# Chunked attention on one core: the order of one head's scores, a unit of values and the softmax steps in the first head of each later group

## The chip, the core and the metric

The kernel runs on one core of a Trainium2 chip. The core has five engines with their own instruction streams: TensorE (PE in the profile, its weight loads PEld) multiplies matrices into PSUM banks, VectorE (DVE) and ScalarE (ACT) read and write PSUM and SBUF, GpSimd (POOL) works on SBUF only, and SyncE (SP) issues most transfers. The engines wait for each other by semaphores. The metric is the device time of one execution in microseconds, as the median of several runs.

## What is computed

Two model blocks follow each other on 512 positions of width 1024. The second one ends with an attention layer of 16 heads of 64 columns and an MLP. Only the attention layer is touched:

```python
q, k, v = jnp.split(h @ w_in, 3, axis=-1)          # 16 heads of 64 columns
def one_chunk(c):                                   # 64 queries, band of 576 keys
    s = jnp.einsum('bqhd,bkhd->bhqk', qb, kb).astype(jnp.float32) * scale + bias[None]
    s = jnp.where(valid[None, None, None, :], s, -jnp.inf)
    p = jax.nn.softmax(s, axis=-1).astype(vb.dtype)
    return jnp.einsum('bhqk,bkhd->bqhd', p, vb)
...
return o @ w_out
```

## The kernel before

The program is one hand-ordered instruction list for each engine; no planner orders anything. It has six phases (a mixer, a gated FFN, retention, an MLP, attention, an MLP). Every fp32 matrix product is done as three matmuls on halves: high by high, low by high, high by low (L629 to L631, helper `product`). ScalarE makes the high half of a block of weights (`w_hi`, L1101) and GpSimd the low half (`w_lo`, L605).

In the attention phase the heads go in four groups of four. A *unit* is a stretch of such products on TensorE: a qk unit gives 128 columns of q or k (24 matmuls of 512 columns), a v unit gives values for half of the positions (48 matmuls of 256 columns). The units of the next group are spread over the heads of the current one, and between them stand three smaller pieces for each head:

- `scores(h + 1)` on TensorE (L973, L975): four tiles of scores, two matmuls each, in the order 0, 2, 3, 1. Tile 0 first waits until the scores of head h have been taken. Tile 1 goes to bank 6 and first waits (semaphore `pt_ready`) until VectorE has finished the low halves of the transposed probabilities of head h - 1 (`probs_lo`), since their source is in bank 6.
- `mix(h - 1)` on TensorE (L1002, L1004), the probabilities of head h - 1 times the values.
- `turn(h)` on TensorE (L991), ten transposes of the probabilities of head h. The last two go to bank 6 and wait until VectorE has taken the scores of head h + 1.

VectorE does `maxima` (L2191, L2195: adds the bias, takes the row maximum), `normalise` (L2199, L2204), `probs_lo` (L2210, `probs_t_lo` in the profile), takes over each unit (`qk_taken` L1790, `qk_lo` L2181, for values `value_lo` L2164), adds the mixed halves (`mixed_add` L2215) and makes their low half (`mixed_lo` L2221). ScalarE does `exps` (L1482), `probs_hi` (L1491), `qk_hi` (L1446, L1447), the high half of the values in `v_unit` (L1472), `mixed_copy` (L1497), `mixed_hi` (L1502) and the weights' high halves. With `normalise(h + 1)` and `exps(h + 1)` in the list of head h, `probs_lo(h)` comes after both.

Each head h has one turn in the loops. The first head of a later group (h = 4, 8 and 12; `s == 0` in the code) has two units, the last qk unit and the first v unit; the second head has the second v unit and a qk unit, the third and fourth have one qk unit each. In the last group, output units (`unit4_narrow`, L629 with `hid_hi`) take the place of the qk units. `unit4_narrow` starts only when every unit before it has been taken.

Of the kernel before, what the change touches and what calls it, by code (L numbers as in the profile page):

```python
# [163 lines left out]
def build(nc, phases, x_in, w_in, w_out, w_gate, w_up, w_down, ret_w_in, ret_w_out, att_w_in,  # L164
# [4 lines left out]
    with ctx:  # L169
# [453 lines left out]
        def _(pe):  # L623
# [213 lines left out]
            for f in phases:  # L837
# [108 lines left out]
                if f == "att":  # L946
# [7 lines left out]
                    def unit4_narrow(n):  # L954

                        unit4(H, 0, fresh=0, bank0=0)
# [64 lines left out]
                    for h in range(1, ATT_HEADS):  # L1021
                        s, last_group = h % 4, h >= ATT_HEADS - 4
                        if s == 0:
                            qk_unit(3)
                            unit_v(X)
                            scores(h + 1)
                            mix(h - 1)
                            turn(h)
                            continue
                        if s == 1 and h > 1:  # L1030
                            unit_v(X)
                            v_units = c.unit.n
                        if last_group and s == 1:
                            scores(h + 1)
                            pe.wait_ge(mix_ready, 8)
                            unit4_narrow(s - 1)
                        else:
                            if last_group:
                                unit4_narrow(s - 1)
                            else:  # L1040
                                qk_unit(s - 1)
                            if h + 1 < ATT_HEADS:
                                scores(h + 1)
                        if s == 1:
                            pe.wait_ge(unit_taken, v_units)
                        mix(h - 1)
                        turn(h)
# [16 lines left out]
        def _(act):  # L1064
# [173 lines left out]
            for f in phases:  # L1238
# [193 lines left out]
                if f == "att":  # L1432
# [89 lines left out]
                    for h in range(1, ATT_HEADS):  # L1522
                        s, last_group = h % 4, h >= ATT_HEADS - 4
                        if s == 0:
                            qk_unit(3)
                            mixed_copy(h - 1)
                            v_unit(0)
                            exps(h + 1)
                            probs_hi()
                            mixed_hi(h - 1)  # L1530
                            continue
                        if s == 1 and h > 1:
                            v_unit(1)
                        if last_group and s == 1:
                            exps(h + 1)
                            after_unit()
                            mixed_copy(h - 1)
                        else:
                            if last_group:
                                after_unit()  # L1540
                            else:
                                qk_unit(s - 1)
                            mixed_copy(h - 1)
                            if h + 1 < ATT_HEADS:
                                exps(h + 1)
                        probs_hi()
                        mixed_hi(h - 1)
# [15 lines left out]
        def _(dve):  # L1563
# [257 lines left out]
            for f in phases:  # L1821
# [330 lines left out]
                if f == "att":  # L2152
# [99 lines left out]
                    for h in range(1, ATT_HEADS):  # L2252
                        s, last_group = h % 4, h >= ATT_HEADS - 4
                        if s == 0:
                            qk_taken(3)
                            maxima(h + 1)
                            qk_lo(3)
                            mixed_add(h - 1)
                            value_lo()
                            normalise(h + 1)  # L2260
                            probs_lo()
                            mixed_lo(h - 1)
                            continue
# [89 lines left out]
```

## Time and profile before

| what | us |
|---|---|
| median of 3 runs | 1879.1 (1878.47 to 1879.91) |
| the profiled execution | 1879.74 |
| its span in the trace | 1878.0 |
| attention's first matmul piece on scores to its last mix | 1307 to 1501 |

The profile is of one execution. A timeline row gives the start, the duration, the engine, the source line, the operation with what it writes and reads, and in brackets how long the engine was idle before it and what ended that. Starts of matmuls that follow each other without a wait are closer than their durations, since matmuls overlap: the distance of two starts is what a matmul costs TensorE, and 128x256 ones start 0.12 us apart, 128x512 ones 0.23 us apart.

### The profile page before, as it was taken

The page shows a single profiled execution, that of the slowest core. Times are in us where ns is not written, and L with a number is a line of the kernel's source. Part 1 is how long each engine was busy: PE and PEld are TensorE (multiplying, and loading weights), DVE is VectorE, ACT ScalarE, POOL GpSimd, SP SyncE. Part 2 cuts the span into 40 slices and gives each one's busy share as a digit, 9 for nine tenths or more (in the row PEclk, how much of TensorE's full clock was granted, in tenths as well). Part 3 has the DMA queues.
Part 4 walks back from the last instruction along what each step waited for, and adds up shares of the span by engine and source line. Part 5 has one row for each costly group of instructions (what it writes and reads, how often), then busy time and mean ns, then how long its engine had stood idle before and what let it go on. Part 6 is the DMA issues. An engine that isn't in the chain of part 4 may idle for free.

```text
span 1878.0 us, 25366 instructions
## 1 busy us (share of the span) xinstructions
PE 1851.3 (99%) x10114; PEld 1608.1 (86%) x10114; DVE 1131.9 (60%) x1807; ACT 848.9 (45%) x1319; POOL 945.9 (50%) x408
## 2 busy tenths in 40 slices
PE   8999999999999999999999999999999999999997
PEld 6778889898888888888889899898888889898987
DVE  5997775775776333433665545357877766354455
ACT  5335443342354232333454535445666546444453
POOL 4573466475443434433347566574223338475653
PEclk9999999999999999999999999999999999999998
DMA  5222414424232222222244141413333252422301
GB/s 185 90 90 68 136 66 144 159 72 154 68 113 68 94 87 90 82 78 88 90 157 135 46 155 48 148 31 118 83 107 106 79 174 74 135 91 90 133 3 45
DMA packets 143041, 186.66 MB, mean 99 GB/s; under 512 B 4016, under 2 KB 102592, under 8 KB 142800
## 3 DMA queue, kind: packets, MB, share of 16 engines
q1 hardware_dynamic: 134848, 170.67, 27.8%
q10 hardware_dynamic: 8080, 14.44, 2.7%
q8 instruction: 77, 1.26, 0.3%
q14 instruction: 36, 0.29, 0.0%
HBM read 178.76 MB, written 6.33 MB: 99 GB/s over the span
## 4 chain that ended last, share of the span: by engine, by line
PE 83%; DVE 8%; ACT 2%; issue 1%; ACTq 0%; DVEq 0%
PE ps L629 27%; PE ps L631 27%; PE ps L630 27%; DVE ps L1852 1%; ACT work L1482 1%; DVE diagonals L1607 1%; DVE xl L1633 0%; DVE work L2204 0%; DVE probs_t_lo L2210 0%; DVE work L2191 0%; PE ps L991 0%; DVE work L1790 0%; PE ps L925 0%; ACT w_hi L1101 0%; DVE q_hi L2181 0%
## 5 line engine op out<-in xcount | busy, mean ns | idle before, releaser
L605 POOL TENSOR_TENSOR w_lo<-raw,w_hi 128x1024 fp32r<-128x1024 f32 x228 | 553.0, 2431 | 752.7 <-ACT w_hi L1101 752.7
L629 PE MATMUL ps<-xh,w_hi 128*128 128x512 f32 x1408 | 554.7, 394 | 3.4 <-DVE xl L1633 1.3
L631 PE MATMUL ps<-xh,w_lo 128*128 128x512 f32 x1408 | 548.7, 390 | 0.0
L630 PE MATMUL ps<-xl,w_hi 128*128 128x512 f32 x1408 | 548.6, 390 | 0.0
L1101 ACT ACTIVATE w_hi<-raw 128x1024 fp32r<-128x1024 f32 x248 | 259.7, 1057 | 409.0 <-PE ps L631 400.8
L629 PEld LDWEIGHTS ps<-xh,w_hi 128*128 128x128 f32 x1408 | 264.7, 188 | 62.8 <-issue 8.0
L631 PEld LDWEIGHTS ps<-xh,w_lo 128*128 128x128 f32 x1408 | 264.5, 188 | 55.8
L630 PEld LDWEIGHTS ps<-xl,w_hi 128*128 128x128 f32 x1408 | 264.9, 188 | 55.3 <-issue 1.9
L629 PE MATMUL ps<-hid_hi,w_hi 128*128 128x256 f32 (+1 forms) x944 | 300.8, 319 | 1.9 <-DVE att_v L2164 0.8
L631 PE MATMUL ps<-hid_hi,w_lo 128*128 128x256 f32 (+1 forms) x944 | 299.5, 317 | 0.0
L630 PE MATMUL ps<-hid_lo,w_hi 128*128 128x256 f32 (+1 forms) x944 | 299.4, 317 | 0.0
L629 PEld LDWEIGHTS ps<-hid_hi,w_hi 128*128 128x128 f32 x944 | 179.9, 191 | 14.9 <-DVE hid_lo L1796 1.8
L631 PEld LDWEIGHTS ps<-hid_hi,w_lo 128*128 128x128 f32 x944 | 179.9, 191 | 12.0
L630 PEld LDWEIGHTS ps<-hid_lo,w_hi 128*128 128x128 f32 x944 | 180.0, 191 | 11.8 <-issue 0.2
L1761 DVE TENSOR_TENSOR x<-x,ps 128x512 f32<-128x512 f32 x140 | 94.9, 685 | 124.9 <-PE ps L631 124.9
L605 POOL TENSOR_TENSOR w_lo<-down,w_hi 128x1024 fp32r<-128x1024 f32 x40 | 96.4, 2424 | 79.3 <-ACT w_hi L1101 79.3
L631 PE MATMUL ps<-combined,w_lo 128*128 128x256 f32 x480 | 135.8, 283 | 0.0
L630 PE MATMUL ps<-combined,w_hi 128*128 128x256 f32 x480 | 135.8, 283 | 0.0
L629 PE MATMUL ps<-combined,w_hi 128*128 128x256 f32 x480 | 135.8, 283 | 0.0
L605 POOL TENSOR_TENSOR w_lo<-work,w_hi 128x1024 fp32r<-128x1024 f32 x52 | 125.0, 2419 | 17.8 <-ACT w_hi L1101 17.8
L2128 DVE SCALAR_TENSOR_TENSOR work<-ps,r_bc 128x512 f32<-128x512 f32 x64 | 43.6, 690 | 83.3 <-PE ps L631 83.2
L629 PEld LDWEIGHTS ps<-combined,w_hi 128*128 128x128 f32 x480 | 92.1, 192 | 0.4
(252 smaller groups left out, 2805.2 us busy)
## 6 DMA issues: line engine op xcount, KB each, us to landing
raw<-in_mlp_w_dram SPq DMA_DIRECT2D x32, 1024.0 KB, 5.3
raw<-in_ret_w_in_dram SPq DMA_DIRECT2D x24, 1024.0 KB, 5.1
work<-in_mlp_w_dram SPq DMA_DIRECT2D x24, 1024.0 KB, 6.3
raw<-in_att_w_in_dram SPq DMA_DIRECT2D x12, 1024.0 KB, 5.4
raw<-in_w_gate_dram SPq DMA_DIRECT2D x11, 1024.0 KB, 5.4
raw<-in_w_up_dram SPq DMA_DIRECT2D x11, 1024.0 KB, 5.4
raw<-in_w_in_dram SPq DMA_DIRECT2D x10, 1024.0 KB, 5.1
raw<-in_ret_w_out_dram SPq DMA_DIRECT2D x8, 1024.0 KB, 5.1
```

The source lines that it names most:

```text
L605: nc.gpsimd.tensor_tensor(halves_of(wl[:, b % 2, :], half), halves_of(source, half), halves_of(wh[:, b % 2, :], half).bitcast(F32), ALU.su ...
L629: nc.tensor.matmul(o, a[0], b[0], start=first, stop=False, skip_group_check=True)
L630: nc.tensor.matmul(o, a[0], b[1], start=False, stop=False, skip_group_check=True)
L631: return nc.tensor.matmul(o, a[1], b[0], start=False, stop=last, skip_group_check=True)
L1101: nc.scalar.activation(halves_of(wh[:, slot, :], half), source, ACT.Copy).then_inc(w_hi, c.made(w_hi))
L1482: last = nc.scalar.activation(probs[:, h % 2, cut], probs[:, h % 2, cut], ACT.Exp, bias=nmx[:, i:i + 1], accum_out=rs[:, i:i + 1])
L1607: V.reciprocal(rough, root_rows).then_inc(dve_step, c.made(dve_step))
L1761: V.tensor_tensor(tiles, tiles, ps[:, where, :].rearrange("p (m c) -> p m c", m=2), ALU.add).then_inc(unit_taken, c.made(unit_taken))
L1852: V.scalar_tensor_tensor(total if last else acc, src, w, acc, ALU.mult, ALU.add).then_inc(signal, c.made(signal))
L2128: V.scalar_tensor_tensor(hval[:, u % 2, :], bank(), 0.0, r_bc[:, :], ALU.max, ALU.mult).then_inc(unit_taken, c.made(unit_taken))
```

## The change

In the turn of the first head of a later group, `scores(h + 1)` moves on TensorE from behind the v unit to between the qk unit and the v unit. On ScalarE `exps(h + 1)`, with the two bias loads that it issues where there is a head h + 5, moves ahead of `mixed_copy(h - 1)` and `v_unit(0)`. On VectorE `normalise(h + 1)` moves ahead of `mixed_add(h - 1)` and `value_lo()`. No instruction is added or removed. It applies to h = 4, 8 and 12.

```diff
@@ tensor @@
                         if s == 0:
                             qk_unit(3)
+                            scores(h + 1)
                             unit_v(X)
-                            scores(h + 1)
                             mix(h - 1)
                             turn(h)
@@ scalar @@
                             qk_unit(3)
+                            exps(h + 1)
                             mixed_copy(h - 1)
                             v_unit(0)
-                            exps(h + 1)
                             probs_hi()
@@ vector @@
                             qk_taken(3)
                             maxima(h + 1)
                             qk_lo(3)
+                            normalise(h + 1)
                             mixed_add(h - 1)
                             value_lo()
-                            normalise(h + 1)
                             probs_lo()
```

TensorE before, in the turn of head 4, from the end of the v unit (L631) over the scores of head 5 (`k_odd`, `q_lo` are the tiles that hold an odd head's k and q) to the first matmul of the mix of head 3:

```order
L631 MATMUL ps<-w_hi,xl 128x256
L973 MATMUL ps<-k_odd,q_lo 128x128 [waits s_taken]
L975 MATMUL ps<-k_odd,q_lo 128x128
L973 MATMUL ps<-k_odd,q_lo 128x384
L975 MATMUL ps<-k_odd,q_lo 128x384
L973 MATMUL ps<-k_odd,q_lo 128x512
L975 MATMUL ps<-k_odd,q_lo 128x512
L973 MATMUL ps<-k_odd,q_lo 128x256 [waits pt_ready]
L975 MATMUL ps<-k_odd,q_lo 128x256
L1002 MATMUL ps<-probs_t_hi,att_v 128x512 [waits pt_ready,mix_added]
```

TensorE after, in the same turn, from the end of the qk unit (L631 with 512 columns) to the start of the v unit (L629 with 256):

```order
L631 MATMUL ps<-xh,w_lo 128x512
L973 MATMUL ps<-k_odd,q_lo 128x128 [waits s_taken]
L975 MATMUL ps<-k_odd,q_lo 128x128
L973 MATMUL ps<-k_odd,q_lo 128x384
L975 MATMUL ps<-k_odd,q_lo 128x384
L973 MATMUL ps<-k_odd,q_lo 128x512
L975 MATMUL ps<-k_odd,q_lo 128x512
L973 MATMUL ps<-k_odd,q_lo 128x256 [waits pt_ready]
L975 MATMUL ps<-k_odd,q_lo 128x256
L629 MATMUL ps<-w_hi,xh 128x256 [waits unit_taken,w_lo]
```

The eight matmuls and their two waits stand 48 matmuls earlier, and the whole v unit now stands behind them.

VectorE before, in the same turn, from the negated maxima of head 5 (L2195) to the low halves of the transposed probabilities of head 4 (L2210):

```order
L2195 TENSOR_SCALAR cols<-cols 128x4 [waits s_taken]
L2181 TENSOR_TENSOR k_parts<-work,k_parts 64x512 [waits unit_taken,hi_made]
L2181 TENSOR_TENSOR k_odd<-work,k_odd 64x512
L2215 TENSOR_TENSOR work<-ps,work 64x512 [waits mix_copied]
L2164 SCALAR_TENSOR_TENSOR att_v<-ps,cols,att_v 128x4x64 [waits hi_made,unit_done]
L2164 SCALAR_TENSOR_TENSOR att_v<-ps,cols,att_v 128x4x64
L2199 RECIPROCAL cols<-cols 128x4 [waits curve_made]
L2204 TENSOR_SCALAR work<-work,cols 128x128 [waits dve_step]
L2204 TENSOR_SCALAR work<-work,cols 128x256
L2204 TENSOR_SCALAR work<-work,cols 128x384
L2204 TENSOR_SCALAR work<-work,cols 128x512
L2210 TENSOR_TENSOR probs_t_lo<-ps,probs_t_hi 128x512 [waits hi_made] x2
```

VectorE after, the same stretch:

```order
L2195 TENSOR_SCALAR cols<-cols 128x4 [waits s_taken]
L2181 TENSOR_TENSOR k_parts<-work,k_parts 64x512 [waits unit_taken,hi_made]
L2181 TENSOR_TENSOR k_odd<-work,k_odd 64x512
L2199 RECIPROCAL cols<-cols 128x4 [waits curve_made]
L2204 TENSOR_SCALAR work<-work,cols 128x128 [waits dve_step]
L2204 TENSOR_SCALAR work<-work,cols 128x256
L2204 TENSOR_SCALAR work<-work,cols 128x384
L2204 TENSOR_SCALAR work<-work,cols 128x512
L2215 TENSOR_TENSOR work<-ps,work 64x512 [waits mix_copied]
L2164 SCALAR_TENSOR_TENSOR att_v<-ps,cols,att_v 128x4x64 [waits hi_made,unit_done]
L2164 SCALAR_TENSOR_TENSOR att_v<-ps,cols,att_v 128x4x64
L2210 TENSOR_TENSOR probs_t_lo<-ps,probs_t_hi 128x512 [waits hi_made] x2
```

The five instructions of `normalise` stand three places earlier, ahead of the two steps that wait for the mix and the v unit. All that precedes L2195 on VectorE, `probs_lo(3)` among it, stands where it stood.

## Rows read from the trace of the kernel before

**Rows 1.** The page, part 1: busy time, share of the span and instructions by engine.
```profile
PE 1851.3 (99%) x10114; PEld 1608.1 (86%) x10114; DVE 1131.9 (60%) x1807; ACT 848.9 (45%) x1319; POOL 945.9 (50%) x408
```

**Rows 2.** The page, part 4: the chain that ended last, shares by engine.
```profile
PE 83%; DVE 8%; ACT 2%; issue 1%; ACTq 0%; DVEq 0%
```

**Rows 3.** Waits of PE, 1300 to 1520 us: total us, times, longest us.
```profile
PE ps L991 <- DVE cols L2191: 2.3, 7, 0.5
...
PE ps L973 <- DVE probs_t_lo L2210: 0.7, 2, 0.4
```

**Rows 4.** Timeline of PE, head 1: scores of head 2, then the mix.
```profile
1322.99 0.22 PE L973 MATMUL ps<-k_parts,q_hi 128*128 128x128 f32 x1
...
1324.50 0.39 PE L973 MATMUL ps<-k_parts,q_hi 128*128 128x256 f32 x1 [0.31 <-DVE probs_t_lo L2210]
...
1324.85 0.40 PE L1002 MATMUL ps<-probs_t_hi,att_v 128*128 128x512 f32 x1
```

**Rows 5.** Timeline of DVE in the same stretch: `probs_lo(0)`.
```profile
1322.83 1.62 DVE L2210 TENSOR_TENSOR probs_t_lo<-ps,probs_t_hi 128x512 fp32r<-128x512 f32 x3
```

**Rows 6.** Timeline of PE, head 4: starts of v unit, scores and mix.
```profile
1352.88 0.28 PE L629 MATMUL ps<-w_hi,xh 128*128 128x256 f32 x1
...
1358.63 0.23 PE L973 MATMUL ps<-k_odd,q_lo 128*128 128x128 f32 x1
...
1359.90 0.39 PE L1002 MATMUL ps<-probs_t_hi,att_v 128*128 128x512 f32 x1
```

**Rows 7.** Timeline of DVE, end of head 3's turn, head 4's, start of head 5's.
```profile
1350.87 2.78 DVE L2181 TENSOR_TENSOR q_lo<-work,q_lo 64x512 fp32r<-64x512 f32 x1
1353.67 0.18 DVE L2199 RECIPROCAL cols<-cols 128x4 f32<-128x4 f32 x1
...
1355.08 1.61 DVE L2210 TENSOR_TENSOR probs_t_lo<-ps,probs_t_hi 128x512 fp32r<-128x512 f32 x3
...
1357.21 0.68 DVE L1790 SCALAR_TENSOR_TENSOR work<-ps,r_bc 128x512 f32<-128x512 f32 x1
1359.51 0.29 DVE L2191 CUSTOM_DVE_ANT_0 work<-ps,work 128x128 f32<-128x128 f32 x1 [1.63 <-PE ps L975]
...
1373.66 0.69 DVE L1790 SCALAR_TENSOR_TENSOR work<-ps,r_bc 128x512 f32<-128x512 f32 x1 [3.52 <-PE ps L631]
```

**Rows 8.** Timeline of POOL and ACT there, and L2181's durations (ns, min/median/max).
```profile
1347.88 5.22 POOL L605 TENSOR_TENSOR w_lo<-raw,w_hi 128x1024 fp32r<-128x1024 f32 x2 [17.96 <-ACT w_hi L1101]
...
1350.89 0.71 ACT L1482 ACTIVATE work<-work,cols 128x512 f32<-128x512 f32 x1
...
L2181 DVE TENSOR_TENSOR q_lo<-work,q_lo x8: 687/688/2782, 1297.2 to 1449.5; 64x512 fp32r<-64x512 f32 x8
```

**Rows 9.** Timelines of PE (v unit's start) and DVE (`probs_lo(7)`), head 8.
```profile
1402.22 0.28 PE L629 MATMUL ps<-w_hi,xh 128*128 128x256 f32 x1
...
1404.43 1.61 DVE L2210 TENSOR_TENSOR probs_t_lo<-ps,probs_t_hi 128x512 fp32r<-128x512 f32 x3
```

**Rows 10.** Timelines of ACT, DVE and PE, head 13: second v unit taken, output unit.
```profile
1466.88 0.84 ACT L1472 ACTIVATE att_v<-ps,cols 128x256 fp32r<-128x256 f32 x2 [1.22 <-PE ps L631]
...
1467.94 0.88 DVE L2164 SCALAR_TENSOR_TENSOR att_v<-ps,cols,att_v 128x256 fp32r<-128x256 f32 x2
...
1468.96 0.47 PE L629 MATMUL ps<-hid_hi,w_hi 128*128 128x512 f32 x1 [0.85 <-DVE att_v L2164]
```

**Rows 11.** PE's timeline at both ends; last row: one microsecond's busy times and PEclk.
```profile
12.68 0.76 PE L629 MATMUL ps<-xh,w_hi 128*128 128x512 f32 x1 [1.27 <-DVE xl L1633]
...
15.73 0.58 PE L629 MATMUL ps<-xh,w_hi 128*128 128x512 f32 x1
...
1861.66 1.05 PE L753 MATMUL ps<-ones,sum_of_squares 128*128 128x1 f32 x8 [1.57 <-DVE sum_of_squares L1648]
...
1862.00:1863.00 1.00, 1.00 (x10) 1.00 (x9) 0.00 (x0) 0.97 (x3) 0.00 (x0) 0.87 0.00 0
```

## Prediction

> **What bounds the kernel now.** I read the page's busy times first: TensorE is busy for 1851.3 us, 99% of the span, and VectorE for 60% [rows 1]. The chain that ended last agrees, 83% of it being TensorE [rows 2]. So the time changes where TensorE starts or stops waiting, and what VectorE and ScalarE win by themselves is worth nothing. Next the waits of TensorE in the attention phase. Its engine rows give small ones only: 2.3 us in seven waits of the transposes for the maxima, and 0.7 us in two waits of the fourth score tile for `probs_lo` [rows 3]. The reader should look at the second kind, because it is the wait that the change moves. Then the timelines of the stretches around heads 4, 8 and 12. In the turn of head 4 TensorE runs v unit, scores and mix without a wait: 1352.88, 1358.63, 1359.90 [rows 6].
>
> **How the wait on bank 6 is priced.** In the turn of head 1 the scores stand directly behind one qk unit, as the change now has it for heads 4, 8 and 12. They start at 1322.99, their last pair is held until 1324.50, and the mix starts at 1324.85 [rows 4]. What it waited for is `probs_lo(0)`, which started at 1322.83 and took 1.62, so ended at 1324.45 [rows 5]. Two things follow. The last pair of `scores(h + 1)` can't start before `probs_lo(h - 1)` ends, and what stands behind the scores starts 0.40 us after that end. Without a wait the scores cost 1359.90 - 1358.63 = 1.27 us [rows 6].
>
> **TensorE, the scores moved up.** In the turn of head 4 the scores wait for `probs_lo(3)`. That one starts at 1355.08 and ends at 1356.69 [rows 7]. Before, the scores started at 1358.63, and the v unit of 1358.63 - 1352.88 = 5.75 us hid this completely. After the change they start where the v unit started, at 1352.88 [rows 6], and `probs_lo(3)` is still 3.8 us from its end. Nothing ahead of it moves: the turn of head 3 and the two steps in head 4's list before the moved ones are unchanged on all engines. So the v unit starts at 1356.69 + 0.40 = 1357.09 instead of at 1352.88 + 1.27 = 1354.15, and the mix at 1362.84 instead of 1359.90. **Cost: 2.94 us.** In the turn of head 8 `probs_lo(7)` ends at 1404.43 + 1.61 = 1406.04 and the v unit started at 1402.22 [rows 9]: 1406.44 - 1403.49 = 2.95 us. The third group repeats the pattern to within 0.01 us. Sum: 2.94 + 2.95 + 2.94 = **8.8 us**.
>
> **Why `probs_lo(3)` is so late there.** `qk_lo`'s second instruction, ahead of it on VectorE, takes 2.78 us against a median of 0.69, while GpSimd works on two `w_lo` halves from 1347.88 to 1353.10 [rows 7, 8]. This long form is there in all three groups, so I take the long value; the rival below takes the short one.
>
> **The other first wait of the scores**, for the scores of head 4 to be taken, costs nothing: VectorE took them before it made `q_lo` at 1350.87 [rows 7]. What is queued behind the new wait on TensorE is the v unit, the mix of head 3, the transposes of head 4 and everything after; ScalarE's copy of the mixed half and of the values, VectorE's `value_lo` and `probs_lo(4)` wait for these, and come later by the same 2.9 us.
>
> **VectorE and ScalarE, the softmax steps moved up.** VectorE was idle for 1.63 us before the maxima of head 5 at 1359.51, waiting for the scores [rows 7]. After the change the scores are complete some 0.4 us after 1356.69, before `qk_taken` is over at 1357.21 + 0.68 = 1357.89, so the maxima start 1.6 us earlier. `exps(5)` and `normalise(5)` then run while TensorE is in the v unit. Their cover is that unit, which ends at 1362.84. Had they no cover, they would still not be on TensorE's path, because `turn(5)` needs them a whole head later. The two bias loads that `exps` issues on ScalarE's queue are issued earlier, and are used four heads later: nothing. The steps that the softmax passes, `mixed_add(3)` and `value_lo`, wait for the mix and the v unit, which are now 2.9 us later than before, so they don't lose by standing behind. GpSimd's and SP's lists are the same, and what they wait for (`w_hi` after the qk unit, `qk_lo`) is not behind anything moved.
>
> **Is anything paid back?** VectorE is ahead after head 4, but it waits 3.52 us for TensorE at 1373.66, in head 5's turn [rows 7]. From there both keep the same distance as before, and the small waits of heads 6 and 7 stay. The one place where the lead counts is head 13. There the output unit starts at 1468.96 after an idle 0.85 us, because the second v unit must be taken first. ScalarE's part of that ends at 1466.88 + 0.84 = 1467.72, VectorE's starts at 1467.94 because it was busy until then [rows 10]. After the change VectorE has finished the previous head earlier and is free at 1467.72 (as times of before); it starts about 0.05 later, so the gain is 0.17 us, once. At the least it is 0, at the most the whole idle 0.85.
>
> **Sum.** 8.8 - 0.2 = +8.7 us (from unrounded terms). The profiled execution took 1879.74 us with a span of 1878.0; its span becomes 1886.7. It lies 0.6 above the median of the runs shown, so I add the difference to the median: 1879.1 + 8.7 = **1887.8 us**, 0.46% slower.
>
> **Rival 1: TensorE's clock falls in the new waits.** Each leaves TensorE idle for about 2.7 us, from the sixth score matmul to the seventh. The longest idle before a dense stretch in the attention phase is now 0.85. At the end of the program the granted clock went from the 2.4 GHz level towards the 1.2 GHz level (0.87 in the microsecond from 1862) after 1.57 us of idleness and one microsecond of one-column matmuls [rows 11]. That is nearly as long, so I can't exclude it. Price: after the start TensorE worked at the lower level from 12.68 to 15.73 [rows 11], 3.05 us, half of which is lost: 1.5 us for each fall. One to three falls give 1889.3 to 1892.3. Against it: the idle stretch lies between full ones, and the one at the end didn't.
> The Trainium skill says in "TensorE: Matmul & The Clock Gate", Part 1, that the array's clock is gated by how busy TensorE has been; it would speak for this rival if the wait counts as idleness enough, and the sum would be by it what this rival says.
>
> **Rival 2: the held instruction is free.** If GpSimd's work no longer met `q_lo` (2.78 to 0.69), VectorE would next wait for the exponentials, whose last one ends at 1350.89 + 0.71 = 1351.60 and its accumulator some 0.1 later [rows 8]. The reciprocal would come at about 1351.8 instead of 1353.67, and `probs_lo` 1.9 us earlier [rows 7]. Cost per group 1.0, sum 3.1 - 0.2: 1882.0 us, too little to be told from no change. Against it: neither engine's work is moved ahead of that point.
> The Trainium skill, "SBUF — State Buffer", section "Who interferes with whom", says that GpSimd and a VectorE instruction with two SBUF inputs exclude each other for the whole instruction, and that whoever starts first holds the port. The trace agrees in the length of `q_lo`. By that rule the order of starts decides, so a small shift of GpSimd could turn it; this is the same 1882.0.
>
> **Rival 3, not slower: the wait at bank 6 finds its data ready.** The place is L973's fourth tile. If the count that it waits for were reached by `probs_lo(2)`, or `probs_lo(3)` ended before about 1353.9, nothing would be held, and only the 0.17 of head 13 would be left: 1878.9 us. The point from which the result could be told from no change (0.2% or 3.8 us, about what a measurement of this kernel can tell) is 1.3 us lost per group, thus `probs_lo(3)` ending at 1355.1 instead of 1356.69. Against it: the code counts heads 0 to h - 1 for the scores of h + 1, and the wait of head 1 ended 0.05 us after `probs_lo(0)` did [rows 4, 5].
> For a real gain the waits of the transposes for the maxima would have to go too, and no more than 2.3 us of them exist [rows 3].
>
> **Chances.** Forecast 0.76 (1886.5 to 1889), rival 1 0.12, rival 2 0.06, rival 3 0.06 (0.02 of it with a gain). Slower by over 0.2%: 0.76 + 0.12 + 0.02 (a rival 2 with only some groups free) = 0.90; within: 0.04 + 0.04 = 0.08; faster 0.02. The range takes in the forecast with a reach of 2 us down for the 0.40 and the restart, and most of rival 1: 1885.5 to 1891.5.
>
> **What the profile of the changed kernel would show.** Right: in the turns of heads 4, 8 and 12 the fourth tile of the scores (L973, 128x256) starts 2.8 us behind its neighbour, released by `probs_t_lo` L2210, and the PE waits for L2210 grow by about 8 us in three waits; the maxima of heads 5, 9 and 13 follow `qk_taken` without idleness; the v unit has no wait before it but this one. Rival 1: PEclk below 1.00 right behind those waits, and 512-column matmuls that start further apart than before. Rival 2: `q_lo` at 0.69 in heads 3, 7 and 11. Rival 3: no PE wait there. The forecast is wrong if `probs_lo(3)` doesn't end at 1356.7, or if the transposes of head 4 start waiting, which I expect not.

## The result

The changed kernel is slower. Before, the median of 4 runs is 1879.51 us (1878.47 to 1880.65); changed, it is 1891.56 us (1889.5 to 1893.55, 4 runs). The ratio is 1.0062, with a 95% interval from 1.0051 to 1.0074: 12 us more. The forecast was 1887.8 us with a range of 1885.5 to 1891.5, so the sign is right and the size is 3.8 us short; the median lies 0.06 us above the range, and as a rise above the kernel before (12.05 us, where the range stood for 6.4 to 12.4) inside it. The executions of the changed kernel also spread more than those before: 4.1 us against 2.2.

The profiled execution took 1889.5 us with a span of 1887.7. Its page, parts 1 and 4 (busy time, share of the span and instructions; then the shares of the chain that ended last):

```profile
PE 1852.3 (98%) x10114; PEld 1608.6 (85%) x10114; DVE 1128.2 (60%) x1807; ACT 849.2 (45%) x1319; POOL 948.2 (50%) x408
...
PE 83%; DVE 8%; ACT 2%; issue 1%; ACTq 0%; DVEq 0%
```

TensorE's busy time grew by 1.0 us against [rows 1] and the span by 9.7, so nearly all of the loss in this execution is TensorE not working. Its waits over the whole execution (total us, times, longest us):

```profile
PE ps L973 <- DVE probs_t_lo L2210: 8.6, 5, 2.7
...
PE ps L991 <- DVE cols L2191: 2.4, 7, 0.5
```

The wait of the fourth score tile for `probs_lo` went from 0.7 us in two times to 8.6 in five; the waits of the transposes stayed [rows 3]. The timeline of TensorE in the turn of head 4 (start, us, engine, line, operation, and in brackets the idle time before it):

```profile
1353.49 0.22 PE L973 MATMUL ps<-k_odd,q_lo 128*128 128x128 f32 x1
...
1354.30 0.40 PE L975 MATMUL ps<-k_odd,q_lo 128*128 128x512 f32 x1
1357.38 0.38 PE L973 MATMUL ps<-k_odd,q_lo 128*128 128x256 f32 x1 [2.68 <-DVE probs_t_lo L2210]
...
1357.71 0.28 PE L629 MATMUL ps<-w_hi,xh 128*128 128x256 f32 x1
```

The v unit starts at 1357.71, which is 4.22 us after the scores' start at 1353.49 where 1.27 would do without a wait [rows 6]: 2.95 us lost. The same wait is 2.67 us long in heads 8 and 12. VectorE's timeline shows what it waited for:

```profile
1351.49 2.78 DVE L2181 TENSOR_TENSOR q_lo<-work,q_lo 64x512 fp32r<-64x512 f32 x1
1354.31 0.18 DVE L2199 RECIPROCAL cols<-cols 128x4 f32<-128x4 f32 x1
...
1355.71 1.61 DVE L2210 TENSOR_TENSOR probs_t_lo<-ps,probs_t_hi 128x512 fp32r<-128x512 f32 x3
1357.24 0.67 DVE L2221 TENSOR_TENSOR hid_lo<-work,hid_hi 64x512 fp32r<-64x512 f32 x1
1357.84 0.68 DVE L1790 SCALAR_TENSOR_TENSOR work<-ps,r_bc 128x512 f32<-128x512 f32 x1
1358.44 0.27 DVE L2191 CUSTOM_DVE_ANT_0 work<-ps,work 128x128 f32<-128x128 f32 x1
```

These are [rows 7], some 0.63 us later, as TensorE's rows are here too. `probs_lo(3)` ends at 1357.32, and TensorE goes on 0.06 later. The maxima of head 5 now follow `qk_taken` without the 1.63 us of idleness.

The second part of the loss stands behind the wait of head 8. TensorE's timeline from there, with the v unit's 256-column matmuls:

```profile
1409.64 0.39 PE L973 MATMUL ps<-k_odd,q_lo 128*128 128x256 f32 x1 [2.67 <-DVE probs_t_lo L2210]
...
1409.98 0.28 PE L629 MATMUL ps<-w_hi,xh 128*128 128x256 f32 x1
...
1410.33 0.34 PE L629 MATMUL ps<-w_hi,xh 128*128 128x256 f32 x1
1410.46 0.42 PE L630 MATMUL ps<-w_lo,xh 128*128 128x256 f32 x1
1410.67 0.42 PE L631 MATMUL ps<-w_hi,xl 128*128 128x256 f32 x1
...
1413.86 0.28 PE L631 MATMUL ps<-w_hi,xl 128*128 128x256 f32 x1
1413.98 0.28 PE L629 MATMUL ps<-w_hi,xh 128*128 128x256 f32 x1
...
1417.21 0.40 PE L1002 MATMUL ps<-probs_t_hi,att_v 128*128 128x512 f32 x1
```

Matmuls start 0.12 us apart at first, then 0.21 from 1410.46 on, and 0.12 again from 1413.86. One microsecond of each, as busy times of the engines, then the granted clock (the third number from the end):

```profile
1409.00:1410.00 1.00, 0.36 (x3) 0.36 (x4) 1.00 (x3) 0.00 (x0) 0.00 (x0) 1.00 0.01 4
...
1411.00:1412.00 1.00, 1.00 (x7) 1.00 (x7) 1.00 (x5) 0.99 (x2) 0.00 (x0) 0.50 0.00 0
```

So the clock fell from the 2.4 to the 1.2 GHz level after TensorE had idled 2.67 us. The v unit, from its start at 1409.98 to the first matmul behind it at 1417.21, took 7.23 us instead of 5.75: 1.48 us. In heads 4 and 12 of this execution it did not fall.

**A measure without the ends of the program.** The start of the program and its last sixteen microseconds vary by themselves from execution to execution. To compare traces I take the time from the first matmul of the attention phase to the first one-column matmul at the end; before, the two starts are 1276.76 (below) and 1861.66 [rows 11], 584.90 us. There is one trace of the kernel before, so this reference is a single execution. First before, then two of the changed kernel:

```profile
1276.76 0.47 PE L629 MATMUL ps<-xh,w_hi 128*128 128x512 f32 x1 [0.87 <-issue]
```

```profile
1277.59 0.47 PE L629 MATMUL ps<-xh,w_hi 128*128 128x512 f32 x1 [0.87 <-issue]
...
1872.43 1.05 PE L753 MATMUL ps<-ones,sum_of_squares 128*128 128x1 f32 x8 [1.57 <-DVE sum_of_squares L1648]
```

Changed, that is 594.84 us: 9.94 more, of which 1.48 are the fall of the clock and 8.46 the rest. The forecast's sum for the rest was 8.66. The table has every profiled kernel read in this way; "falls" are the v or output units of which a part ran at the lower level in that trace. The last column takes off what that cost: in a v unit its length above 5.75 us (1.48 in most), in the output unit of head 13 its length above that of the run with the normalising alone (1.6 with the softmax steps alone, 1.85 with the exponentials alone).

| kernel | median us (its before) | attention's start to end part, against 584.90 | falls seen | without them |
|---|---|---|---|---|
| the change | 1891.56 (1879.51) | +9.94 | 1 | +8.46 |
| the change again | 1892.65 (1879.55) | +11.54 | 2 | +8.58 |
| wait filled with work | 1887.52 (1879.55) | +8.53 | 0 | +8.53 |
| scores alone | 1890.30 (1879.55) | +9.99 | 1 | +8.5 |
| softmax steps alone | 1881.83 (1879.55) | +3.80 | 1 | +2.2 |
| three tiles alone | 1879.59 (1880.20) | -0.04 | 0 | -0.04 |
| probs_lo first | 1884.80 (1880.20) | +4.17 | 0 | +4.17 |
| longer wait | 1895.63 (1880.20) | +16.43 | 3 | +12.0 |
| mixed_lo deferred | 1875.45 (1880.20) | -3.43 | 0 | -3.43 |
| probs_lo first, filled | 1885.40 (1879.92) | +4.40 | 0 | +4.40 |
| exponentials alone | 1886.34 (1879.92) | +6.65 | 1 | +4.8 |
| normalising alone | 1881.39 (1879.92) | +2.17 | 0 | +2.17 |
| probs_lo first, again | 1885.04, one execution (1879.57) | +4.25 | 0 | +4.25 |

### The profile page after: what moved, and what is told of

Its sections match the earlier page's. It is cut to its first block, busy times and chain, and to the rows that moved or that the text cites. A ratio compares the mean times of both kernels' runs of the same rounds, so it can differ in the third digit from the quotient of the medians.

```text
span 1887.7 us, 25366 instructions
## 1 busy us (share of the span) xinstructions
PE 1852.3 (98%) x10114; PEld 1608.6 (85%) x10114; DVE 1128.2 (60%) x1807; ACT 849.2 (45%) x1319; POOL 948.2 (50%) x408
## 4 chain that ended last, share of the span: by engine, by line
PE 83%; DVE 8%; ACT 2%; issue 1%; ACTq 0%; DVEq 0%
PE ps L629 27%; PE ps L630 27%; PE ps L631 27%; DVE ps L1852 1%; DVE probs_t_lo L2210 1%; DVE work L2204 1%; ACT work L1482 1%; DVE diagonals L1607 1%; DVE xl L1633 0%; PE ps L991 0%; PE ps L925 0%; DVE work L2191 0%; ACT w_hi L1101 0%; DVE work L1790 0%; DVE q_hi L2181 0%
## 5 line engine op out<-in xcount | busy, mean ns | idle before, releaser
L629 PE MATMUL ps<-xh,w_hi 128*128 128x512 f32 x1408 | 554.6, 394 | 4.3 <-DVE xl L1633 2.1
L631 PE MATMUL ps<-xh,w_lo 128*128 128x512 f32 x1408 | 548.6, 390 | 0.0
L629 PEld LDWEIGHTS ps<-xh,w_hi 128*128 128x128 f32 x1408 | 264.8, 188 | 63.5 <-issue 8.0
L631 PEld LDWEIGHTS ps<-xh,w_lo 128*128 128x128 f32 x1408 | 264.7, 188 | 55.4
L629 PE MATMUL ps<-hid_hi,w_hi 128*128 128x256 f32 (+1 forms) x944 | 300.8, 319 | 1.8 <-DVE att_v L2164 0.7
L631 PE MATMUL ps<-hid_hi,w_lo 128*128 128x256 f32 (+1 forms) x944 | 299.5, 317 | 0.0
L629 PEld LDWEIGHTS ps<-hid_hi,w_hi 128*128 128x128 f32 x944 | 179.9, 191 | 14.8 <-DVE hid_lo L1796 1.8
L631 PEld LDWEIGHTS ps<-hid_hi,w_lo 128*128 128x128 f32 x944 | 179.9, 191 | 12.0
L631 PE MATMUL ps<-combined,w_lo 128*128 128x256 f32 x480 | 135.8, 283 | 0.0
L629 PE MATMUL ps<-combined,w_hi 128*128 128x256 f32 x480 | 135.8, 283 | 0.0
L629 PEld LDWEIGHTS ps<-combined,w_hi 128*128 128x128 f32 x480 | 92.1, 192 | 0.4
```

The lines of the kernel that those rows point to most:

```text
L629: nc.tensor.matmul(o, a[0], b[0], start=first, stop=False, skip_group_check=True)
L631: return nc.tensor.matmul(o, a[1], b[0], start=False, stop=last, skip_group_check=True)
```

## The experiments

**The change again, and with the waits filled.** The first question was whether the 3.8 us above the forecast are the clock. The changed kernel was run again, and beside it a version in which TensorE multiplies into a bank that is free there while it waits:

```diff
+                            if i == 1 and filled:
+                                pe.wait_ge(mix_added, h - 2)
+                                for _ in range(filled):
+                                    nc.tensor.matmul(ps[:, 7, :], q[:, 0:P], k_hi[:, 0:SEQ],
+                                                     start=True, stop=True, skip_group_check=True)
                             if i == 1 and h >= 2:
                                 pe.wait_ge(pt_ready, pt_before_att + len(TURNED) * (h - 1))
...
                             qk_unit(3)
-                            scores(h + 1)
+                            scores(h + 1, filled=11)
```

> The change again, beside the runs of the kernel before. Theory A (each of three waits on bank 6 costs TensorE 2.9 us, and in some executions the granted clock falls in one to three of them, at 1.5 us each): 1888 to 1893 us with a spread of several us between executions, lowest near 1888.5, against 1879 to 1880 before. Theory B (the 3.8 us that the result lies above the forecast are a constant cost that the trace doesn't show): all executions within 1.5 us of each other, near 1891.5.

Measured: 1892.65 us (1889.16 to 1895.26, 5 runs), ratio 1.0067 [1.0053, 1.0081]. The spread of 6.1 us fits theory A and rules B out. This trace has two falls, in the v units of heads 4 and 12 (7.23 and 7.24 us), where the first had one, in head 8. The traced execution is the fastest of its five. The mean granted clock goes with the time: 0.995 and 0.996 at 1889.16 and 1889.66 us, 0.994 at 1892.65 and 1892.66, 0.992 at 1895.26.

> The change, with eleven extra 128x512 matmuls into the free bank 7 on TensorE between the third and the fourth tile of the moved scores, so that TensorE works through the wait instead of idling. The wait for the probabilities is as long as before, so the cost of the wait itself stays. Theory A (the executions above the forecast are falls of the granted clock in the idle waits): no falls, 1887.5 to 1888.5 us, with a spread below 1.5 us, and the clock of the mean execution as high as before. Theory B (the extra is no matter of the clock): the same median as the change itself, within 0.7 us.

Measured: 1887.52 us (1885.99 to 1889.31, 5 runs), ratio 1.0043 [1.0029, 1.0056]. The filled stretch in the turn of head 4, on TensorE (lines are 5 higher in this kernel; L974 is the filler):

```profile
1352.78 0.39 PE L980 MATMUL ps<-k_odd,q_lo 128*128 128x512 f32 x1
1353.01 2.73 PE L974 MATMUL ps<-k_odd,q_lo 128*128 128x512 f32 x11
1355.85 0.38 PE L978 MATMUL ps<-k_odd,q_lo 128*128 128x256 f32 x1
```

The fourth tile comes as late as before, 3.07 us behind its neighbour, but TensorE isn't idle. The granted clock stays at 1.00 over the whole attention phase, all three v units take 5.75 us, and the median falls by 5.1 us, to the forecast; the mean granted clock of its executions is 0.996 or 0.997. The wait's own cost stays, +8.5 us in the trace, so what the filling gives back is time at the lower clock. Its size is less sure: three falls at 1.48 us would be 4.4, not 5.1, and the program's ends are in the medians too. The spread, 3.3 us, is above the 1.5 expected; what it holds is told with the two groups below.

**One part of the change at a time.** TensorE's part alone, that is the diff's first hunk:

> Only TensorE's part of the change: the scores ahead of the v unit; ScalarE and VectorE keep the order of before. Theory A (the wait of the fourth tile is the whole cost and the order of the softmax steps doesn't count): within 0.5 us of the change in the trace, the same three waits of 2.7 us, median 1888 to 1893. Rival (the moved softmax steps cost or give something of their own): over 1 us away from the change.

Measured: 1890.3 us (1889.55 to 1890.86), ratio 1.0055 [1.0041, 1.0069]. The waits in its trace, of which the other two are 2.68 us too:

```profile
1357.97 0.39 PE L973 MATMUL ps<-k_odd,q_lo 128*128 128x256 f32 x1 [2.68 <-DVE probs_t_lo L2210]
```

It loses what the whole change loses (+8.5 us without the fall, against 8.46 and 8.58). The moved scores are the whole cost of the waits, and the moved softmax steps add nothing to it in the traces. The medians are less alike: 1890.3 us with a spread of 1.3 here, against 1892.65 with a spread of 6.1 for the whole change beside it. The waits are as long in both, so whether the softmax steps make the falls more frequent, or five executions are too few, is open.

ScalarE's and VectorE's part alone, that is the other two hunks:

> Only ScalarE's and VectorE's part: exponentials and normalising of head h + 1 ahead of the values' parts; TensorE keeps the order of before. Theory A: no wait of TensorE is added, at most the 0.17 us of head 13 are gained: 1878.9 to 1879.6 us, the same as before. Rival (the part costs something because normalise now blocks mixed_add and value_lo behind it): 1 us or more slower.

Measured: 1881.83 us (1880.52 to 1885.0, 11 runs), ratio 1.0015 [1.0006, 1.0024]: slower by 2.3 us, where I expected no change. Its trace has waits of TensorE that neither other kernel has: 0.25 us before the qk unit of heads 5 and 9, and these two in head 13:

```profile
1470.96 0.39 PE L973 MATMUL ps<-k_parts,q_hi 128*128 128x256 f32 x1 [0.64 <-DVE probs_t_lo L2210]
...
1472.68 0.47 PE L629 MATMUL ps<-hid_hi,w_hi 128*128 128x512 f32 x1 [1.22 <-DVE att_v L2164]
```

One candidate for the reason is in ScalarE's timeline in the turn of head 4. The first row is the first exponential of head 5 with the idle time before it; then come the mixed copy and the values, which are queued behind the exponentials:

```profile
1364.31 0.41 ACT L1482 ACTIVATE work<-work,cols 128x128 f32<-128x128 f32 x1 [2.52 <-DVE cols L2195]
...
1366.63 0.59 ACT L1497 ACTIVATE work<-ps 64x512 f32<-64x512 f32 x1
1367.25 0.84 ACT L1472 ACTIVATE att_v<-ps,cols 128x256 fp32r<-128x256 f32 x2
```

With the scores behind the v unit, the maxima are late, ScalarE idles 2.52 us for them, and the values of the v unit, which the next units wait for, are taken later. The other candidate is VectorE, where the normalising now stands ahead of the values. To see which of the two engines' order costs this, each was moved alone:

> The kernel before with exps(h + 1) ahead of mixed_copy(h - 1) and v_unit(0) on ScalarE in heads 4, 8 and 12, and nothing else moved. It splits the run with the softmax steps alone (2.3 us slower than before), where ScalarE idles 2.5 us for the maxima ahead of exps and mixed_copy and v_unit are queued behind it. Theory A (this queueing on ScalarE is the cost): 1881 to 1882.5 us, as slow as with both parts. Rival (VectorE's part, normalise ahead of mixed_add and value_lo, is the cost): 1879.5 to 1880.3 us, as before.

Measured: 1886.34 us (1885.13 to 1886.88, 6 runs), ratio 1.0034 [1.0021, 1.0046]: 6.4 us slower, far more than either theory said. In its trace `mixed_lo` at the end of head 4's turn, which took 0.69 us, runs while GpSimd works on `w_lo` (1370.93 to 1376.15) and takes 2.80, and VectorE takes the second v unit behind it:

```profile
1371.08 2.80 DVE L2221 TENSOR_TENSOR hid_lo<-work,hid_hi 64x512 fp32r<-64x512 f32 x1
1373.91 0.87 DVE L2164 SCALAR_TENSOR_TENSOR att_v<-ps,cols,att_v 128x256 fp32r<-128x256 f32 x2
```

The same happens in the turn of head 12 (2.75 us). In head 13, where the output unit needs these values at once, TensorE waits 3.28 us, after 1.34 for the fourth score tile. The clock is at the lower level before the second wait is over, and stays there until microsecond 1478:

```profile
1470.74 0.38 PE L973 MATMUL ps<-k_parts,q_hi 128*128 128x256 f32 x1 [1.34 <-DVE probs_t_lo L2210]
...
1474.52 0.77 PE L629 MATMUL ps<-hid_hi,w_hi 128*128 128x512 f32 x1 [3.28 <-DVE att_v L2164]
```

```profile
1472.00:1473.00 1.00, 0.00 (x0) 0.00 (x0) 1.00 (x1) 0.00 (x0) 1.00 (x2) 0.50 0.00 0
```

These two waits, 0.85 before, make 3.8 of the 4.8 us that the table has without the fall. How much of them is the order and how much the long instruction was not told apart.

> The kernel before with normalise(h + 1) ahead of mixed_add(h - 1) and value_lo() on VectorE in heads 4, 8 and 12, and nothing else moved. If ScalarE's queueing is the cost of the softmax steps alone: 1879.5 to 1880.7 us, at most 0.5 us above before. If VectorE's order is the cost: 1881 us or more.

Measured: 1881.39 us (1879.88 to 1884.08, 11 runs), ratio 1.0012 [1.0003, 1.0021]. Its trace has the waits of the softmax run to 0.01 us (0.24 in heads 5 and 9; 0.63 and 1.22 in head 13), with ScalarE's order as before; only the fall behind them is missing. What makes them is on VectorE: it idles for the exponentials, normalises, and takes the first v unit 2.65 us later than before, measured from the transposes of head 4.

```profile
1365.57 0.18 DVE L2199 RECIPROCAL cols<-cols 128x4 f32<-128x4 f32 x1 [1.05 <-ACT work L1482]
...
1367.81 0.88 DVE L2164 SCALAR_TENSOR_TENSOR att_v<-ps,cols,att_v 128x256 fp32r<-128x256 f32 x2
```

So each order costs when it is moved alone, and in each a step that waits was put ahead of steps that free a unit; with both moved the waits are those of VectorE's order.

**The fourth tile by itself.** If the wait on bank 6 is all that costs, the other three tiles can go ahead of the v unit freely:

```diff
-                    def scores(h):
+                    def scores(h, tiles=tuple(SCORES)):
...
-                        for i in SCORES:
+                        for i in tiles:
...
                             qk_unit(3)
+                            scores(h + 1, (0, 2, 3))
                             unit_v(X)
-                            scores(h + 1)
+                            scores(h + 1, (1,))
                             mix(h - 1)
```

> The kernel before, in which three of the four score tiles (0, 2 and 3) of head h + 1 go ahead of the v unit in heads 4, 8 and 12, and only the fourth (tile 1, bank 6) stays behind it; ScalarE and VectorE as before. It differs from the run with the scores alone by that one tile. Theory A (the wait of the tile in bank 6 for probs_lo(h - 1) is the whole cost of moving the scores): no wait of TensorE ahead of the v unit, 1879 to 1880 us, the same as before. Rival (splitting the run of TensorE's work, or the first wait of the scores, costs by itself): over 1 us slower than before.

Measured: 1879.59 us (1879.09 to 1879.88, 11 runs) against 1880.2, ratio 0.9997 [0.9988, 1.0006]; in the trace 0.04 us less than before. Against the scores alone only two matmuls stand elsewhere, and the whole loss is gone.

**Why `probs_lo` is late, and the length of the wait.** The order was changed so that VectorE makes `probs_lo` ahead of the 2.78 us instruction:

```diff
                             mixed_add(h - 1)
+                            if s == 3:
+                                made = c.next(hi_made)
+                                normalise(h + 1)
+                                probs_lo()
+                                qk_lo(s - 1, made=made)
+                                mixed_lo(h - 1)
+                                continue
```

> The change, and in the turns of heads 3, 7 and 11 VectorE normalises head h + 1 and makes probs_lo(h) ahead of the two instructions of qk_lo, of which the second took 2.78 us. Theory A (TensorE waits for the end of probs_lo, which is late because of this instruction): probs_lo ends 1.0 to 1.9 us earlier and the three waits fall from 2.7 to between 0.8 and 1.7 us; 1882 to 1885 us; with idleness that short no fall of the clock, so a spread below 2 us. Rival (probs_lo is late because of what ScalarE does ahead of it): the waits stay above 2.3 us and the time at 1888 or more.

Measured: 1884.8 us (1882.15 to 1885.15, 10 runs), ratio 1.0021 [1.0012, 1.0031]. TensorE's wait in the turn of head 4, and what VectorE does before:

```profile
1355.64 0.39 PE L973 MATMUL ps<-k_odd,q_lo 128*128 128x256 f32 x1 [1.24 <-DVE probs_t_lo L2210]
```

```profile
1352.04 0.18 DVE L2199 RECIPROCAL cols<-cols 128x4 f32<-128x4 f32 x1 [1.63 <-ACT work L1482]
1352.25 1.80 DVE L2204 TENSOR_SCALAR work<-work,cols 128x128 f32<-128x128 f32 x4
1353.97 1.61 DVE L2210 TENSOR_TENSOR probs_t_lo<-ps,probs_t_hi 128x512 fp32r<-128x512 f32 x3
```

The three waits fell from 2.7 to 1.24 us and the loss from 8.5 to 4.2, as theory A says; only the spread, 3.0 us, is above the 2 expected. What holds VectorE then is ScalarE's exponentials (1.63 us idle), as the prediction's rival 2 had it for a free `q_lo`. The normalising also takes 1.80 us instead of 1.28, 0.52 more, which is about what is missing from the gain of 1.9 us that rival 2 worked out.

The other way round, with the wait made longer:

```diff
                             normalise(h + 1)
+                            if s == 3:
+                                for _ in range(2):
+                                    dve.wait_ge(dve_step, c.now(dve_step))
+                                    V.memset(ssq[:, :], 0.0).then_inc(dve_step, c.made(dve_step))
                         probs_lo()
```

> The change with the suspected wait made longer: in heads 3, 7 and 11 VectorE fills a tile that is free there with zeros twice, ahead of probs_lo; no result changes. Theory A (the end of probs_lo sets when TensorE goes on, and the clock falls more often the longer TensorE idles): each of the three waits grows by what the two instructions take, 0.6 to 1.4 us, so 2 to 4 us in sum, and the clock falls in all three waits of each execution: 1894 to 1898 us. Rival (the falls don't depend on the length of the idleness): the falls stay at one or two, 1890 to 1894 us.

Measured: 1895.63 us (1895.35 to 1896.49, 4 runs), ratio 1.0084 [1.0068, 1.0099]. The waits of heads 4, 8 and 12:

```profile
1358.68 0.39 PE L973 MATMUL ps<-k_odd,q_lo 128*128 128x256 f32 x1 [3.81 <-DVE probs_t_lo L2210]
...
1413.58 0.39 PE L973 MATMUL ps<-k_odd,q_lo 128*128 128x256 f32 x1 [3.82 <-DVE probs_t_lo L2210]
...
1468.50 0.58 PE L973 MATMUL ps<-k_odd,q_lo 128*128 128x256 f32 x1 [3.83 <-DVE probs_t_lo L2210]
```

Each wait is 1.14 us longer, and the granted clock is at 0.50 behind all three (microseconds 1360, 1415, 1470). In the third it is there already when the fourth tile starts (0.58 us instead of 0.39). With 3.8 us idle it fell each time in this trace, with 2.7 us in one or two of three in the traces before. The four executions spread by only 1.1 us, which would fit three falls in each; one of them was traced.

**The two groups of executions.** The ten executions with `probs_lo` first lie at 1882.15, 1882.16 and 1883.7 to 1885.15. To see whether this is the clock in its three waits:

> The run with probs_lo ahead of qk_lo, whose executions fell into two groups (1882.2 and 1884.9 us) although its three waits are only 1.24 us long, and in it five extra 128x512 matmuls into bank 7 ahead of the fourth score tile, so that TensorE works through most of each wait. Theory A (the upper group is the granted clock falling behind one of these waits): 1882 to 1883 us with the upper group gone. Rival (the two groups have nothing to do with these waits): two groups again, 1882 to 1885 us.

Measured: 1885.4 us (1882.05 to 1886.33, 9 runs), ratio 1.0028 [1.0018, 1.0038]. None of the three waits is left in its trace, and the executions still go from 1882.05 to 1886.33. Theory A falls, the rival stands. The same kernel without filling, in one more execution:

> One more look at the run with probs_lo ahead of qk_lo, whose executions fall into two groups (1882.2 and 1884.9 us) also where its three waits are filled. If this execution is of the upper group, its row of the granted clock should show one or two more stretches at the lower level than the profile at hand, and where. Theory A: behind the idleness of head 13's turn (0.7 us) or at the start of the program. If it is of the lower group, nothing is told apart.

Measured: 1885.04 us in one run, one of the upper group. Its attention part is +4.25 us where the first trace had +4.17: the same, and no fall anywhere in it. So the falls behind the waits are not the reason. What differs is the end of the program, which begins with matmuls of one column (L753). The second row is the start of the last stretch of matmuls (L730):

```profile
1866.24 1.60 PE L753 MATMUL ps<-ones,sum_of_squares 128*128 128x1 f32 x8 [1.57 <-DVE sum_of_squares L1648]
...
1873.15 3.79 PE L730 MATMUL ps<-diagonals,ones 128*128 128x128 f32 x16 [1.89 <-DVE diagonals L1591]
```

From the first to the second it is 6.91 us here. In the filled run of the change it is 4.73, before it was 6.22 (1867.88 - 1861.66), and in the change's own profile 5.21: up to 2.2 us between executions. The granted clock (third number from the end) goes with it. Two microseconds each, first in this run, 2 us into the stretch, then in the filled run of the change, as far in:

```profile
1868.00:1870.00 2.00, 2.00 (x11) 2.00 (x11) 0.00 (x0) 0.01 (x1) 0.00 (x0) 0.50 0.00 0
```

```profile
1871.00:1873.00 2.00, 1.23 (x12) 1.14 (x11) 0.35 (x3) 0.36 (x2) 0.00 (x0) 0.82 0.00 0
```

Here the clock is at the lower level already, there for the last part alone. The span before the attention phase varies by 2.4 us more (1275.96 to 1278.33). These ends hide or double a small difference in single executions; that is why the table above leaves them out.

They also account for the groups, as far as there are traces. The filled kernel's trace is of an execution at 1882.05 us, the other two are of the upper group, 1884.49 and 1885.04. The attention part is as long in all three (+4.40, +4.17, +4.25). But it starts at 1276.15 against 1277.24 and 1277.09, and the end stretch takes 4.73 us against 6.30 and 6.91: 2.7 and 3.1 us, where the times differ by 2.4 and 3.0. The lower trace is of a slightly different kernel, so this is one step short of a trace of each group of one kernel. The mean granted clock goes along: 0.997 at 1882.15, 1882.16 and 1883.69, 0.995 or 0.996 in the seven others.

**A faster order.** The waits of the transposes for the maxima [rows 3] come from VectorE being late at the start of each turn, because `mixed_lo` of the previous turn stands in front. On the kernel before:

```diff
                             qk_taken(s - 1)
                             maxima(h + 1)
+                            if s in (2, 3):
+                                mixed_lo(h - 2)
...
                         probs_lo()
-                        mixed_lo(h - 1)
+                        if last_group or s == 0:
+                            mixed_lo(h - 1)
```

and, likewise, `mixed_lo(h - 2)` behind `maxima(h + 1)` for `s == 0`.

> Not the change but another order of VectorE on the kernel before: mixed_lo of a head (0.69 us) goes from the end of its turn behind the maxima of the next one, in the turns that have a qk unit at their start. Expected: VectorE takes unit and maxima 0.69 us earlier, so the waits of the transposes for the maxima (0.2 to 0.46 us) and of the fourth score tile for probs_lo (0.1 to 0.7 us lost) get shorter or go: 1876 to 1878.5 us, 1 to 3 us faster than before. Rival (another engine ends these waits too, so that nothing is won): 1879 to 1880 us.

Measured: 1875.45 us (1874.53 to 1878.39, 11 runs) against 1880.2, ratio 0.9977 [0.9968, 0.9986]. In the trace the attention part is 3.43 us shorter, and in the turn of head 3 the ten transposes run through, where before the last two waited:

```profile
1345.03 1.28 PE L991 MATMUL ps<-ident,work 128*128 128x128 f32 x10
1346.07 0.48 PE L629 MATMUL ps<-xh,w_hi 128*128 128x512 f32 x1
```

Before:

```profile
1345.59 1.06 PE L991 MATMUL ps<-ident,work 128*128 128x128 f32 x8
1347.11 0.44 PE L991 MATMUL ps<-ident,work 128*128 128x128 f32 x2 [0.46 <-DVE cols L2191]
1347.30 0.48 PE L629 MATMUL ps<-xh,w_hi 128*128 128x512 f32 x1
```

It is faster than both kernels, and by more than the 1 to 3 us expected (4.75 in the medians, 3.43 in the trace). From the first transpose to the next unit it is 1.04 us where it was 1.71: a wait shown as 0.46 us of idleness cost 0.67 from start to start. Of the seven waits for the maxima that TensorE had in the attention phase, the six of heads 2, 3, 6, 7, 10 and 11 are gone; only that of head 0 is left.

## Why the prediction was right, and where it was short

- **The price of the wait**: right. The rule read off head 1 (what stands behind the scores starts 0.40 us after `probs_lo` ends) gave 2.94 us; measured 2.95 in head 4. The sum of 8.8 less 0.2 for head 13 was 8.7, and the four traces of kernels that hold the moved scores with this wait give 8.46 to 8.58 once the clock's part is off.
- **That the wait is all that the scores cost**: right. The three tiles that don't need it moved for nothing, and taking 1.4 us off each wait took half the loss away.
- **The softmax steps cost nothing**: right for the change, but the reason given, that they would not be on TensorE's path even without cover, is wrong. Without the scores moved up they cost 2.3 us. They are harmless there because the maxima come 1.6 us earlier and the mix 2.9 us later. ScalarE is through with them at 1363.32, before the mix ends (1364.86). VectorE is through at 1365.02 and then still waits 0.50 us for ScalarE's mixed copy, which it needs next.
- **Head 13**: 0.17 us forecast; the output unit's wait went from 0.85 to 0.73, so 0.12.
- **The step that failed** is the weight of rival 1. I took no fall of the clock as the likeliest and gave the falls 0.12, because the idle stretch lies between full ones. Its price (1.5 us each) and its place were right: 1.48 us. But the falls come in every trace that has the idle waits of 2.7 us: one in the first, two in the second, one with the scores alone. With the waits filled there is none, and the median falls by 5.1 us. The median of the change is 12.05 us above before, 3.5 above the 8.5 of the waits. If that were all falls, it would be 2.4 in a typical execution; this is worked out and not counted, and the program's ends vary by 2.4 and 2.2 us beside it. The execution at 1895.26 lies 6.1 us above a traced one with two falls, so one more fall can't fill it; where the rest of its low clock (0.992) stood is open.
- **The price of a fall** came out right from a stretch that shows it less plainly than the prediction says. From 12.68 to 15.73 the starts of the 512-column matmuls lie 0.42 to 0.61 us apart instead of 0.23, but the profile's granted clock reads 1.00 in those microseconds. The slow pace is shown there, its reason is not.
- **The ceiling on a gain** was too low. Rival 3 had no more than 2.3 us in the waits of the transposes; taking six of the seven away gave 3.43 us, because a wait costs more than the idleness shown for it.
- Rivals 2 and 3 did not happen: `q_lo` took 2.78 us in the changed kernel too.

The Trainium skill says in "TensorE: Matmul & The Clock Gate", Part 1, that the array's clock is gated by how busy TensorE has been. The traces agree in that every fall in the attention phase stands at or behind a wait, and none came where the waits were filled. In these traces it fell at four of nine waits of 2.7 us and at three of three of 3.8 us.

## What to carry to other kernels

Before moving a block ahead of a long unit, read for each wait in the block when its releaser ends now: a wait that costs nothing today may be hidden only by the unit that the block is moved past. Price it from start to start of what stands around it, since the idleness shown for it is less (2.68 us shown, 2.95 lost). A block with several waits can be split, and the part whose data is ready moves freely. A step that waits long, put ahead of steps that free a buffer, costs by what is queued behind it, even on engines that are half idle. And where TensorE is the bound, an added wait of 2 to 3 us has to be priced with the lower clock behind it, 1.5 us here each time it falls.

## What the runs showed of the hardware

The granted clock fell after single idle stretches of 2.67 to 2.70 us in an otherwise full stream, and not after each of them: 4 of 9 in three traces (two of the changed kernel, one with the scores alone). In the run with the softmax steps alone it fell behind two waits of 0.64 and 1.22 us that lie close together (1470.96 and 1472.68), so idleness needs not be in one piece. The run with the normalising alone has the same two waits (0.63 and 1.22 us) and no fall, so there too the wait does not decide it alone. Single waits of 1.22 to 1.24 us had none in six cases. A fall kept TensorE at the 1.2 GHz level for some 3.4 us and cost 1.5 to 1.6 us; in the run with the exponentials alone it stayed there for some 7 us, 3 of them idle, and cost 1.85. Instructions of VectorE that run while GpSimd makes `w_lo` can take 2.8 us instead of 0.7, and which instruction it hits moves with the order of others (`q_lo` in the changed kernel, `mixed_lo` in the run with the exponentials alone).
